# Attention units of a three-kind encoder layer dealt from two streams instead of one

## The chip, the cores and the metric

The kernel runs on one core of one Trainium2 chip. The metric is the device time of one launch in microseconds (us). Before the change the median of three runs is 3494.93 us (3491.45 to 3495.29).

## The reference

Two layers (DEPTH = 2) process a prompt of 1024 tokens and 8 samples of 16 new tokens each, 128 new tokens with 256 past positions a sample: 1152 rows of width 1024. A layer is `x += concat[A(h), B(h), C(h)] @ w_out` with `h = RMSNorm(x)`, and then `x += SwiGLU(RMSNorm(x))`.

One projection of h feeds three kinds of heads, all with normalised q and k:

- A: six query heads on two key/value heads, width 64, a window of the own 64-token chunk and two before it, a learned sink, a bias by distance. Its past is 128 keys.
- B: four differential heads. Each has two softmax maps of width 32; weights are `p0 - lam * p1`; the result is normalised per head. All keys up to the own chunk, a bias by distance, 256 past keys.
- C: six heads, width 64, causal, with cumulative log forget gates added to the scores, 256 past keys.

All arithmetic is float32. The kernel splits operands of its large products into a high and a low part and adds three products.

## The kernel before, in words

After `setup`, a loop over the two layers calls four phases, each with its own tiles, semaphores and a barrier at its end: `project`, `attend`, `mix` and `feed`. The residual x (128 partitions x 9 token tiles x 1024, 4.72 MB) stays in SBUF from `setup` to the end.

`project` (L438) works through 54 units (six column blocks of w_in, nine token tiles each). In each unit PE adds 24 products, ACT squares, DVE norms; two units later PE turns q and k (`turn_rows`), ACT takes the high part out of PSUM (`take_turned`), DVE the low part (`cut_turned`), and SP stores both to `qkT_hi` and `qkT_lo` in DRAM (`store_turned`, L508). The tiles t_hi and t_lo have two buffers each: ACT waits for the stores of two units ago before it writes again. All DMAs of the kernel are issued by SP, in the order of the program.

`attend` (L819) works in groups of two heads: A (three groups), B (two), C (three). A group's head h has nine units, one per token tile; the ninth (i = 8) is the sample tile. So there are 144 units in one row: all of A, all of B, all of C. The engines run in a lock step over iterations u. In iteration u, PE computes the scores of unit u (`score`), turns the weights of unit u-2 (`turn`), turns past keys or finished outputs if any are due (`turn_extra`), multiplies unit u-3 with the values (`values`) and turns a sample's output back (`turn_back`). DVE adds the bias and finds the minimum (`front`), for B also joins the two maps (`back`). ACT takes the exponent (`exps`) and moves what PE turned out of PSUM (`evacuate`, `evacuate_extra`). Each stage has two buffers.

What sets the order of loads is SP's program (L976 to L998): for each group the past keys, past values and sample queries of the next group (`load_past`), then q and k of two heads ahead (`load_qk`, three sets of buffers), then bias rows and values (`load_front`), then the store of the finished group (`mixT`). A wait of SP for a free buffer holds back all that stands behind it. POOL zeroes `qpast` once a group. A's groups j = 0, 1, 2 hold heads j and j+3, so each of the three groups loads and turns the past keys of both key/value heads.

`mix` (L1307) loads, for eight steps g, a stripe of mixT and of w_out, splits them on ACT and DVE, and PE adds step g into eight PSUM banks; then PE does ten more sums with all stripes at hand, and DVE adds the sums to x. The raw tiles have two buffers. `feed` is the gated layer, and takes over half of the time.

Of the kernel before, what the change touches and what calls it, by code (L numbers as in the profile page):

```python
# [437 lines left out]
def project(nc, t, k, layer):  # L438
# [29 lines left out]
    scaled_q, f_sum, f_abs, f_exp, f_ln, f_out, f_stored, rolled = (  # L468
        ph.sem(n) for n in ("scaled_q", "f_sum", "f_abs", "f_exp", "f_ln", "f_out", "f_stored", "rolled"))
# [25 lines left out]
    with nc.Block() as block:  # L495
        @block.sync
        def _(sp):
# [41 lines left out]
            for u, (b, i) in enumerate(work):  # L539
# [27 lines left out]
            sp.wait_ge(rolled, 32)  # L567
            sp.wait_ge(f_stored, 32)
# [217 lines left out]
class Group:  # L786


    def __init__(self, index, kind, j):
        self.index, self.kind, self.j = index, kind, j  # L790
        self.D = B_DIM if kind == "B" else HEAD
        self.maps = P // self.D
        self.per_head = self.maps // 2
        self.packed = P // self.D
        self.nb = DEC_BATCH // self.packed
        self.halves = 1 if kind == "A" else PAST // P
        self.n_past = self.halves * P
        self.n_samp = self.n_past + P
        self.width = 2 * P if kind == "A" else SEQ
        self.tile = {"A": 0, "B": 3, "C": 5}[kind] + j  # L800

        self.q_row = {"A": lambda m: (j + 3 * m) * HEAD, "B": lambda m: 512 + j * P + m * B_DIM,
                      "C": lambda m: 1024 + j * P + m * HEAD}[kind]
        self.k_row = {"A": 384, "B": 768 + j * P, "C": 1408 + j * P}[kind]
        self.v_col = {"A": VA, "B": VB + j * P, "C": VC + j * P}[kind]
        self.past_chunks = self.maps * self.nb * self.halves // 4
# [10 lines left out]


def attend(nc, t, k, layer):  # L819

    ph = Phase(nc, "att")
    groups = [Group(n, kind, j) for n, (kind, j) in enumerate(
        [("A", 0), ("A", 1), ("A", 2), ("B", 0), ("B", 1), ("C", 0), ("C", 1), ("C", 2)])]
    NG, UG = len(groups), 2 * T
    NH = 2 * NG
# [7 lines left out]
    oT, mixTb = ph.sb("oT", [HEAD, P]), ph.sb("mixTb", [P, TOK])

    units = [(g, h, i) for g in groups for h in range(2) for i in range(T)]
    NU = len(units)
    jobs_to = [0]
    for g, h, i in units:
        jobs_to.append(jobs_to[-1] + g.per_head)
    NJ = jobs_to[-1]  # L840
# [6 lines left out]
    sub_sq = ph.sb("sub_sq", [P, T, P])  # L847
    sub_ms, sub_root = ph.sb("sub_ms", [P, UG]), ph.sb("sub_root", [P, UG])
# [3 lines left out]
    add_in, v_in = ([ph.sem(f"{n}{i}") for i in range(2)] for n in ("add_in", "v_in"))  # L852
    kp_in, vp_in, qpast_zeroed, qpast_in, const_in = (
        ph.sem(n) for n in ("kp_in", "vp_in", "qpast_zeroed", "qpast_in", "const_in"))
    prepared, masked, scored, biased, exped, sink_ready, inv_ready, weighed = (
        ph.sem(n) for n in ("prepared", "masked", "scored", "biased", "exped", "sink_ready", "inv_ready", "weighed"))
    turned, evacuated, multiplied, taken_out = (
        ph.sem(n) for n in ("turned", "evacuated", "multiplied", "taken_out"))
    steps, sub_squared, sub_mean, sub_rooted, sub_done, mix_stored = (
        ph.sem(n) for n in ("steps", "sub_squared", "sub_mean", "sub_rooted", "sub_done", "mix_stored"))  # L860

    extra = {}
    for g in groups:
        for c in range(g.past_chunks):
            extra.setdefault(g.index * UG + 2 + c, []).append(("past", g, c))
        for c in range(3):
            extra.setdefault((g.index + 1) * UG + 7 + c, []).append(("mix", g, c))
    N_ITER = NU + 11
    order = []
    for u in range(N_ITER):  # L870
        if 2 <= u <= NU + 1:
            g, h, i = units[u - 2]
            order += [("p", u - 2, c) for c in range(g.n_chunks(i))]
        order += [(what, g.index, c) for what, g, c in extra.get(u, [])]
        if 3 <= u <= NU + 2 and units[u - 3][2] == TP:
            order.append(("new", u - 3, 0))
        if 4 <= u <= NU + 3 and units[u - 4][2] == TP:
# [4 lines left out]
    inv_to = [sum(x[0].kind == "B" or x[2] >= TP - 1 for x in units[:u]) for u in range(NU + 1)]  # L882
    sinks_to = [sum(x[0].kind == "A" and x[2] >= TP - 1 for x in units[:u]) for u in range(NU + 1)]
    n_qk = {"A": 6, "B": 8, "C": 6}
    n_add = {"A": 4, "B": 4, "C": 6}

    def to(g, parity, count):

        return 16 * sum(count(x) for x in groups[:g.index + 1] if parity is None or x.index % 2 == parity)

    def qk_to(hh):

        return 16 * sum(n_qk[groups[x // 2].kind] for x in range(hh % SETS, hh + 1, SETS))

# [3 lines left out]
    def span_of(u):  # L898

        g, h, i = units[u]  # L900
        a = jobs_to[u - i]
        return slice(a, a + TP * g.per_head, g.per_head) if i < TP else slice(jobs_to[u], jobs_to[u] + 1)

    with nc.Block() as block:
        @block.sync
        def _(sp):
# [3 lines left out]
            def load_qk(hh):  # L910

                g, h, b = groups[hh // 2], hh % 2, hh % SETS
                sem, D = qk_in[b], g.D
                if hh >= SETS:
                    sp.wait_ge(scored, jobs_to[(hh - SETS + 1) * T])
                if g.kind == "B":
                    for r, (of_k, of_q) in enumerate(((hi, hi), (lo, hi), (hi, lo), (lo, lo))):
                        own = slice(r * D, (r + 1) * D)
                        for x, src, row in ((0, of_k, g.k_row + 2 * h * D), (1, of_q, g.q_row(2 * h))):
                            sp.dma_start(qk[own, b, x:4:2, :].bitcast(F32), src[row:row + 2 * D, :].rearrange("(m d) n -> d m n", d=D)).then_inc(sem, 16)  # L920
                else:
                    for x, row, parts in ((0, g.k_row + h * D, (hi, lo)), (1, g.q_row(h), (hi, hi)), (2, g.q_row(h), (lo, lo))):
                        for r in range(2):
                            sp.dma_start(qk[r * D:(r + 1) * D, b, x, :].bitcast(F32), parts[r][row:row + D, :]).then_inc(sem, 16)

            def load_front(g):

                b, j, kind, sem = g.index % 2, g.j, g.kind, add_in[g.index % 2]
                if g.index >= 2:
                    sp.wait_ge(biased, jobs_to[(g.index - 1) * UG])  # L930
                for h in range(2):
                    if kind == "A":
                        sp.dma_start(add_p[:, b, h, 0:g.width], t["bias_a"][j + 3 * h]).then_inc(sem, 16)
                        sp.dma_start(add_s[:, b, h, 0:g.n_samp], t["bias_sa"][j + 3 * h]).then_inc(sem, 16)
                    elif kind == "B":
                        sp.dma_start(add_p[:, b, h, :], t["bias_b"][2 * j + h]).then_inc(sem, 16)
                        sp.dma_start(add_s[:, b, h, :], t["bias_sb"][2 * j + h]).then_inc(sem, 16)
                    else:
                        head = slice(2 * j + h, 2 * j + h + 1)
                        sp.dma_start(add_p[:, b, h, :], t["cum_prompt"][head, :].broadcast_to([P, SEQ])).then_inc(sem, 16)  # L940
                        past = t["cum_past"].rearrange("(b h) n -> b h n", h=C_HEADS)[:, head, :]
                        sp.dma_start(add_s[:, b, h, 0:PAST], past.broadcast_to([DEC_BATCH, DEC_SEQ, PAST])).then_inc(sem, 16)
                        sp.dma_start(add_s[:, b, h, PAST:g.n_samp], t["cum_new"][head, :].broadcast_to([P, P])).then_inc(sem, 16)
                if g.index >= 2:
                    sp.wait_ge(multiplied, (g.index - 1) * UG)
# [706 lines left out]
```

## Time and profile before

| what | value |
|---|---|
| median of three runs | 3494.93 us |
| profiled execution | 3499.59 us, span 3498.1 us |
| granted TensorE clock, mean over the span | 0.945 |
| busy: PE, DVE, ACT, POOL | 90%, 46%, 31%, 0% |
| moved by DMA | 335.7 MB, 96 GB/s over the span |

The span is the profiled stretch on the core; the execution's own time is 1.5 us longer. PE's busy time includes pipelined matmuls, so a busy PE is not PE at its peak. The first layer's phases lie at about 80 to 419 us (project), 419 to 822 (attend), 822 to 932 (mix) and from there to about 1780 (feed); the second layer repeats them. The granted clock is TensorE's, as a share of full speed; 1.00 is 2.4 GHz, 0.50 is 1.2 GHz.

### The profile page before, as it was taken

The page shows a single profiled execution, that of the slowest core. Times are in us where ns is not written, and L with a number is a line of the kernel's source. Part 1 is how long each engine was busy: PE and PEld are TensorE (multiplying, and loading weights), DVE is VectorE, ACT ScalarE, POOL GpSimd, SP SyncE. Part 2 cuts the span into 40 slices and gives each one's busy share as a digit, 9 for nine tenths or more (in the row PEclk, how much of TensorE's full clock was granted, in tenths as well). Part 3 has the DMA queues.
Part 4 walks back from the last instruction along what each step waited for, and adds up shares of the span by engine and source line. Part 5 has one row for each costly group of instructions (what it writes and reads, how often), then busy time and mean ns, then how long its engine had stood idle before and what let it go on. Part 6 is the DMA issues. An engine that isn't in the chain of part 4 may idle for free. (4 is left out here: it accounts for less than half of the span.)

```text
span 3498.1 us, 48824 instructions
## 1 busy us (share of the span) xinstructions
PE 3143.7 (90%) x17938; PEld 2884.2 (82%) x17938; DVE 1592.4 (46%) x3178; ACT 1070.4 (31%) x2279; POOL 15.4 (0%) x20
## 2 busy tenths in 40 slices
PE   0699788898899999999968996889898999999999
PEld 0588787787799999999957896778777999999998
DVE  0455236633244545445446452483234454454454
ACT  1332166663321111111123223576524111111112
POOL 0000000000000000000000000000000000000000
PEclk9899878998999999999989998789998999999999
DMA  7255586753021111111024557866322111111111
GB/s 171 86 173 160 174 201 151 184 131 116 20 65 36 54 36 36 54 36 36 24 90 145 162 185 173 183 161 152 108 82 67 37 36 54 36 36 54 36 36 61
DMA packets 417475, 335.70 MB, mean 96 GB/s; under 512 B 132578, under 2 KB 376238, under 8 KB 417274
## 3 DMA queue, kind: packets, MB, share of 16 engines
q1 hardware_dynamic: 417306, 333.53, 35.1%
q8 instruction: 96, 1.57, 0.2%
q14 instruction: 73, 0.60, 0.1%
HBM read 238.31 MB, written 96.97 MB: 96 GB/s over the span
## 5 line engine op out<-in xcount | busy, mean ns | idle before, releaser
L1560 DVE TENSOR_TENSOR x<-x,ffn_down 128x512 f32<-128x512 f32 x792 | 509.5, 683 | 0.0
L1582 DVE TENSOR_TENSOR ffn_xn<-ffn_xn,ffn_up 128x384 f32<-128x384 f32 x132 | 73.1, 554 | 758.0 <-ACT ffn_xn L1527 758.0
L408 PE MATMUL ffn_up<-ffn_h_hi,ffn_hi_g 128*128 128x384 f32 x1056 | 360.5, 341 | 15.0 <-DVE ffn_h_lo L233 10.4
L410 PE MATMUL ffn_up<-ffn_h_hi,ffn_lo_g 128*128 128x384 f32 x1056 | 359.8, 341 | 0.0
L409 PE MATMUL ffn_up<-ffn_h_lo,ffn_hi_g 128*128 128x384 f32 x1056 | 359.2, 340 | 0.0
L408 PE MATMUL ffn_up<-ffn_h_hi,ffn_hi_u 128*128 128x384 f32 x1056 | 355.3, 336 | 3.2 <-DVE ffn_lo_u L233 3.2
L410 PE MATMUL ffn_up<-ffn_h_hi,ffn_lo_u 128*128 128x384 f32 x1056 | 354.9, 336 | 0.0
L409 PE MATMUL ffn_up<-ffn_h_lo,ffn_hi_u 128*128 128x384 f32 x1056 | 354.9, 336 | 0.0
L1527 ACT ACTIVATE ffn_xn<-ffn_up 128x384 f32<-128x384 f32 x132 | 64.9, 491 | 861.1 <-PE ffn_up L410 861.1
L408 PE MATMUL prj_acc<-prj_w_hi,prj_h_hi 128*128 128x384 f32 (+2 forms) x864 | 322.1, 373 | 3.1 <-DVE prj_w_lo L233 3.0
L409 PE MATMUL prj_acc<-prj_w_lo,prj_h_hi 128*128 128x384 f32 (+2 forms) x864 | 312.4, 362 | 0.0
L410 PE MATMUL prj_acc<-prj_w_hi,prj_h_lo 128*128 128x384 f32 (+2 forms) x864 | 311.9, 361 | 0.0
L408 PE MATMUL ffn_down<-ffn_hi_d,ffn_a_hi 128*128 128x512 f32 x792 | 308.3, 389 | 0.0
L409 PE MATMUL ffn_down<-ffn_lo_d,ffn_a_hi 128*128 128x512 f32 x792 | 308.2, 389 | 0.0
L410 PE MATMUL ffn_down<-ffn_hi_d,ffn_a_lo 128*128 128x512 f32 x792 | 308.2, 389 | 0.0
L1034 PE MATMUL att_S<-att_qk 128*128 128x256 f32 (+3 forms) x672 | 196.8, 394 | 72.3 <-DMA att_qk<-scratch_qkT_lo 55.9
L1097 PE MATMUL att_O<-att_vn,att_pT 128*128 128x64 f32 x1800 | 250.8, 284 | 0.0
L1141 ACT ACTIVATE att_p<-att_s,att_bias 128x128 f32<-128x128 f32 (+3 forms) x360 | 241.9, 674 | 13.9 <-DVE att_bias L1238 12.8
L1238 DVE CUSTOM_DVE_ANT_0 att_s<-att_S,att_add_p 128x128 f32<-128x128 f32 (+3 forms) x224 | 164.8, 755 | 178.5 <-PE att_S L1037 123.9
L1097 PEld LDWEIGHTS att_O<-att_vn,att_pT 128*128 128x128 f32 x1800 | 245.9, 209 | 0.0
L1155 ACT ACTIVATE att_pT<-att_TR 128x256 f32<-128x256 f32 (+3 forms) x368 | 158.3, 453 | 197.5 <-PE att_TR L1059 195.5
L408 PEld LDWEIGHTS ffn_up<-ffn_h_hi,ffn_hi_g 128*128 128x128 f32 x1056 | 202.5, 192 | 18.4 <-DVE ffn_h_lo L233 11.6
(172 smaller groups left out, 5156.3 us busy)
## 6 DMA issues: line engine op xcount, KB each, us to landing
att_qk<-scratch_qkT_hi SPq DMA_DIRECT2D x104, 288.0 KB, 6.6
att_qk<-scratch_qkT_lo SPq DMA_DIRECT2D x104, 288.0 KB, 8.5
ffn_raw_g<-in_w_gate SPq DMA_DIRECT2D x44, 512.0 KB, 4.0
ffn_raw_u<-in_w_up SPq DMA_DIRECT2D x44, 512.0 KB, 5.1
ffn_raw_d<-in_w_down SPq DMA_DIRECT2D x44, 512.0 KB, 5.0
scratch_qkv<-prj_nat SPq DMA_DIRECT2D x72, 192.0 KB, 1.9
prj_w_raw<-in_w_in SPq DMA_DIRECT2D x64, 192.0 KB, 2.7
scratch_qkv<-prj_nat SPq DMA_DIRECT2D x36, 256.0 KB, 2.1
```

What stands on the lines that cost most here:

```text
L408: pe.matmul(out, l_hi, r_hi, start=first, stop=False)
L409: pe.matmul(out, l_hi, r_lo, start=False, stop=False)
L410: return pe.matmul(out, l_lo, r_hi, start=False, stop=final)
L1034: last = pe.matmul(out[:, c:c + w], q, kk[:, k0 + c:k0 + c + w], start=(x == 0), stop=(x == len(qs) - 1 and not masked_end))
L1097: last = pe.matmul(O[:, hh % 2, i * HEAD:(i + 1) * HEAD], pT[:, u % 2, x * P:(x + 1) * P], vn[:, b, kt, v], start=(x == 0), stop=(x == len ...
L1141: act.activation(p[:, u % 2, r, 0:n], s[:, job % 2, 0:n], ACT.Exp, bias=bias[:, job:job + 1], scale=-1.0, accum_out=total[:, job:job + 1]) ...
L1155: act.activation(pT[:, u % 2, c * 512:c * 512 + w], TR[:, n % 2, 0:w], ACT.Copy).then_inc(evacuated, 1)
L1238: dve.tensor_tensor_reduce(s[:, job % 2, 0:n], S[:, job % 2, 0:n], extra_row, -1.0, lowest, ALU.add, ALU.min, bias[:, job:job + 1]).then_i ...
L1527: act.activation(sg[:, b, :], up[:, b, 0, 0:384], ACT.Silu).then_inc(activated, 1)
L1560: dve.tensor_tensor(x, x, down[:, (q * ND + n) % 4, :], ALU.add).then_inc(added, 1)
L1582: dve.tensor_tensor(a32[:, b, :], sg[:, b, :], up[:, b, 1, 0:384], ALU.mult).then_inc(gated, 1)
```

## The change

- `Group` becomes `Head`: 16 heads, 0 to 5 of A, 6 to 9 of B, 10 to 15 of C. Heads 2p and 2p+1 form pair p, whose output is one stripe of mixT. A's pairs are neighbours now, so mixT has the order of the reference, and w_out is loaded in one piece in every step of `mix`.
- `two_streams` deals the 144 units: stream 0 holds A's 54, stream 1 B's 36 and then C's 54. Each unit has a weight; the units are sorted by the share of their stream's weight that lies ahead of them.
- A's six heads form one bundle: values, past keys and past values are loaded once, and past keys turned once in a layer. B and C have a bundle per pair. The turned past keys (`kpT`), past values (`vp`), output columns (`O`) and `mixn` have one place a stream, the raw past keys (`kp`) and `mixTb` one in all; q and k still have three sets. `qpast` has four, and is zeroed once in a layer.
- For A and C, the low part of q is multiplied with the high part of k alone (64 rows); the low-by-low product and its load are left out.
- SP's order is planned: each load is listed at the unit whose end frees its buffer (-1: at once), and the loads of one unit are sorted by the unit that needs them.
- vn, mixn, sub_sq and mixTb lie in x's place in SBUF. `project` stores x to DRAM in unit 9, `mix` loads it back after the loads of step 6.

```diff
+        t["x_kept"] = nc.dram_tensor("scratch_x_kept", (P, T, D_MODEL), F32).ap()
...
                 if u >= 1 and NORMED[work[u - 1][0]]:
                     store_turned(order[u - 1])
+                if u == T:
+                    sp.dma_start(t["x_kept"], k["x"][:]).then_inc(x_kept, 16)
...
+    def weight(self, i):
+
+        return 3.5 * self.halves if i == TP else self.n_cols(i) / P * 0.45 + 0.1
+
+
+def two_streams(heads):
+
+    order = []
+    for stream in range(2):
+        own = [(h, i) for h in heads if h.stream == stream for i in range(T)]
+        whole, at = sum(h.weight(i) for h, i in own), 0
+        for h, i in own:
+            order.append((at / whole, stream, h, i))
+            at += h.weight(i)
+    order.sort(key=lambda e: e[:2])
+    return [(h, i) for _, _, h, i in order]
...
+    spare = k["x"][:].rearrange("p t d -> p (t d)")
+    vn = spare[:, 0:4 * TOK].rearrange("p (s t d) -> p s t d", s=4, t=T)
+    mixn = spare[:, 4 * TOK:6 * TOK].rearrange("p (s t d) -> p s t d", s=2, t=T)
...
+    for h in openers:
+        past_at[h.n] = max(at[h.n, 1], after)
+        after = past_at[h.n] + h.past_chunks + 2
...
+    for h in seconds:
+        mix_at[h.n] = after = max(end[h.n] + 8, after)
...
+    for h in begun:
+        load_at.setdefault(free_at(qk_before[h.n]), []).append((first[h.n], 0, "qk", h))
+        load_at.setdefault(free_at(add_before[h.n]), []).append((first[h.n], 1, "add", h))
+        load_at.setdefault(free_at(q_before[h.n]), []).append((end[h.n], 3, "qpast", h))
+    for n, h in enumerate(openers):
+        v_last = None if v_before[h.bundle] is None else closer[v_before[h.bundle]]
+        load_at.setdefault(free_at(v_last) + 3 * (v_last is not None), []).append((first[h.n], 2, "v", h))
+        kp_free = -1 if n == 0 else past_at[openers[n - 1].n] + openers[n - 1].past_chunks - 1
+        load_at.setdefault(kp_free, []).append((past_at[h.n], 4, "kp", h))
+        vp_last = None if past_before[h.bundle] is None else closer[past_before[h.bundle]]
+        load_at.setdefault(free_at(vp_last) + 3 * (vp_last is not None), []).append((end[h.n], 5, "vp", h))
+    for h in seconds:
+        load_at.setdefault(mix_at[h.n] + 2, []).append((N_ITER, 6, "mix", h))
...
-                    for x, row, parts in ((0, g.k_row + h * D, (hi, lo)), (1, g.q_row(h), (hi, hi)), (2, g.q_row(h), (lo, lo))):
+                    for x, row, parts in ((0, h.k_row, (hi, lo)), (1, h.q_row, (hi, hi)), (2, h.q_row, (lo,))):
...
+                        passes = [(qk[:, b, 1, tok], qk[:, b, 0, :]), (qk[0:HEAD, b, 2, tok], qk[0:HEAD, b, 0, :])]
...
+                    if c == 0 and pair_rank[h.pair]:
+                        act.wait_ge(mix_stored, 16 * pair_rank[h.pair])
...
+                sp.dma_start(w_raw[:, g % 2, :], src[g * P:(g + 1) * P, :]).then_inc(came[g % 2], 16)
+                if g == KD - 2:
+                    sp.dma_start(k["x"][:], t["x_kept"]).then_inc(x_in, 16)
...
+            dve.wait_ge(x_in, 16)
             for u in range(2 * T):
```

## Rows read from the trace of the kernel before

**Rows 1.** Windows by stage: stretch, length, busy by engine, granted clock, DMA share, GB/s.
```profile
429.00:545.00 116.00, 90.28 (x620) 84.53 (x621) 39.90 (x169) 64.97 (x219) 2.85 (x3) 0.75 0.87 199
545.00:649.00 104.00, 91.35 (x623) 79.04 (x622) 81.21 (x215) 73.87 (x183) 0.95 (x1) 0.88 0.74 169
649.00:805.00 156.00, 149.53 (x1228) 134.22 (x1227) 59.48 (x156) 99.58 (x234) 2.86 (x3) 0.98 0.54 131
```
**Rows 2.** Windows of single heads: A, B, B with past keys, two of C.
```profile
447.25:457.23 9.98, 9.98 (x94) 9.66 (x94) 5.46 (x24) 8.58 (x32) 0.38 (x1) 1.00 1.06 252
630.22:656.42 26.20, 23.58 (x183) 19.77 (x183) 22.20 (x64) 20.03 (x54) 0.95 (x1) 1.00 0.76 189
596.87:630.22 33.35, 27.69 (x206) 24.04 (x206) 28.91 (x71) 25.76 (x62) 0.00 (x0) 0.95 0.56 120
711.05:759.50 48.45, 47.37 (x403) 42.79 (x403) 15.32 (x44) 30.52 (x75) 0.95 (x1) 1.00 0.71 173
...
640.00:650.00 10.00, 8.16 (x46) 5.49 (x46) 9.72 (x26) 8.39 (x20) 0.00 (x0) 1.00 0.97 251
```
**Rows 3.** Timeline of PE in attention: start, length, line, operation, count, [idle before, releaser].
```profile
435.77 0.80 PE L1034 MATMUL att_S<-att_qk 128*128 128x256 f32 x2 [5.36 <-DVE att_bias L1238]
...
528.35 0.47 PE L1034 MATMUL att_S<-att_qk 128*128 128x128 f32 x2
...
537.25 1.09 PE L1073 MATMUL att_TR<-ident,att_kp 128*128 128x128 f32 x4 [5.22 <-DMA att_kp<-in_cache_b_k]
```
**Rows 4.** Waits, 419 to 822 us: total, times, longest.
```profile
PE att_S L1034 <- DMA att_qk<-scratch_qkT_lo: 28.3, 4, 14.6
```
**Rows 5.** Window of attention's first loads.
```profile
420.00:460.00 40.00, 23.97 (x180) 22.59 (x180) 12.71 (x56) 20.30 (x68) 0.95 (x1) 0.71 1.05 234
```
**Rows 6.** Timeline of SP's queue in attention.
```profile
418.93 0.54 SPq L924 DMA_DIRECT2D att_qk<-scratch_qkT_hi  x1
...
524.36 10.16 SPq L959 DMA_DIRECT2D att_kp<-in_cache_b_k  x8
```
**Rows 7.** DMA issues: count, KB each, median us from issue to landing.
```profile
att_qk<-scratch_qkT_lo SPq DMA_DIRECT2D x104, 288.0 KB, 8.5
...
x<-in_x_prompt SPq DMA_DIRECT2D x1, 4096.0 KB, 13.6
...
scratch_bias_b<-set_tile_b SPq DMA_DIRECT2D x1, 2048.0 KB, 8.7
```
**Rows 8.** Timeline of all engines at the end of attention.
```profile
806.10 0.56 DVE L1238 CUSTOM_DVE_ANT_0 att_s<-att_S,att_add_s 128x384 f32<-128x384 f32 x1 [2.45 <-PE att_S L1045]
...
817.99 0.77 ACT L1168 ACTIVATE att_mixTb<-att_TR 128x512 f32<-128x512 f32 x2 [0.26 <-PE att_TR L1082]
818.77 0.35 SPq L997 DMA_DIRECT2D scratch_mixT<-att_mixTb  x1
822.45 0.32 SPq L1337 DMA_DIRECT2D mix_m_raw<-scratch_mixT  x1
```
**Rows 9.** Timeline of SP's queue in the projection, units 9 and 10.
```profile
209.71 0.65 SPq L517 DMA_DIRECT2D scratch_qkT_lo<-prj_t_lo  x1
...
213.28 0.58 SPq L517 DMA_DIRECT2D scratch_qkT_lo<-prj_t_lo  x1
```
**Rows 10.** Timeline of ACT in the projection.
```profile
220.47 0.38 ACT L228 ACTIVATE prj_t_hi<-prj_turn 128x256 fp32r<-128x256 f32 x1 [1.14 <-DMA scratch_qkT_lo<-prj_t_lo]
...
222.10 0.38 ACT L650 ACTIVATE prj_sq<-prj_acc 128x256 f32<-128x256 f32 x1 [1.15 <-PE prj_acc L410]
...
226.56 0.38 ACT L650 ACTIVATE prj_sq<-prj_acc 128x256 f32<-128x256 f32 x1 [2.48 <-PE prj_acc L410]
```
**Rows 11.** Timeline of ACT in mix, step 7.
```profile
861.51 1.17 ACT L228 ACTIVATE mix_m_hi<-mix_m_raw 128x1152 fp32r<-128x1152 f32 x1 [0.99 <-DMA mix_w_raw<-in_w_out]
```
**Rows 12.** Timeline of DVE in mix, step 7 and the first sums.
```profile
863.99 1.22 DVE L233 TENSOR_TENSOR mix_w_lo<-mix_w_raw,mix_w_hi 128x1024 fp32r<-128x1024 f32 x1
873.02 5.45 DVE L1382 TENSOR_TENSOR x<-x,mix_acc 128x512 f32<-128x512 f32 x8 [7.81 <-PE mix_acc L410]
```

More of the change, by code:

```diff
@@ L819, in attend @@
 def attend(nc, t, k, layer):
     ph = Phase(nc, "att")
[L822 to L825, printed above, removed]
-    SETS = 3
+    heads = [Head(n) for n in range(A_HEADS + B_HEADS + C_HEADS)]
+    units = two_streams(heads)
+    NU, NP = len(units), len(heads) // 2
+    at = {(h.n, i): u for u, (h, i) in enumerate(units)}
+    first, end = ({h.n: at[h.n, i] for h in heads} for i in (0, TP))
@@ new lines, in attend, with rotate @@
+    begun = sorted(heads, key=lambda h: first[h.n])
+    ended = sorted(heads, key=lambda h: end[h.n])
+    openers = [h for h in begun if h.first_of_bundle]
+    closer = {h.bundle: h for h in heads}
+    SETS = 3
+    jobs_to = [0]
+    for h, i in units:
+        jobs_to.append(jobs_to[-1] + h.maps)
+    NJ = jobs_to[-1]
+    column = [sum(T * x.maps for x in heads[:h.n]) + i * h.maps for h, i in units]
+    def rotate(users, slots, start, stop):
+        place, before, last = {}, {}, [None] * slots
+        for x in users:
+            s = min(range(slots), key=lambda s: -1 if last[s] is None else stop(last[s]))
+            place[x.n], before[x.n], last[s] = s, last[s], x
+            assert before[x.n] is None or stop(before[x.n]) < start(x)
+        return place, before
@@ L832, in attend @@
+    qpast = ph.sb("qpast", [P, 4, 4, P])
+    add_p, add_s = ph.sb("add_p", [P, 4, SEQ]), ph.sb("add_s", [P, 4, 3 * P])
     s, p, pT = ph.sb("s", [P, 2, SEQ]), ph.sb("p", [P, 2, 2, SEQ]), ph.sb("pT", [P, 2, SEQ])
[L833 to L840, printed above, removed]
+    oT = ph.sb("oT", [HEAD, P])
@@ L862, in attend @@
[L862 to L865, printed above, removed]
-        for c in range(3):
-            extra.setdefault((g.index + 1) * UG + 7 + c, []).append(("mix", g, c))
-    N_ITER = NU + 11
+    steps, sub_mean, sub_rooted, sub_done, mix_stored = (
+        ph.sem(n) for n in ("steps", "sub_mean", "sub_rooted", "sub_done", "mix_stored"))
+    seconds = [h for h in ended if h.half]
+    extra, sub_at, load_at = {}, {}, {}
@@ L871, in attend @@
         if 2 <= u <= NU + 1:
[L872 to L875, printed above, removed]
+            h, i = units[u - 2]
+            order += [("p", u - 2, c) for c in range(h.n_chunks(i))]
+        order += [(what, h.n, c) for what, h, c in extra.get(u, [])]
+        if 3 <= u <= NU + 2 and units[u - 3][1] == TP:
             order.append(("new", u - 3, 0))
-        if 4 <= u <= NU + 3 and units[u - 4][2] == TP:
+        if 4 <= u <= NU + 3 and units[u - 4][1] == TP:
             order.append(("back", u - 4, 0))
@@ L881, in attend @@
     weighed_to = [sum(x[0].kind == "B" for x in units[:u]) for u in range(NU + 1)]
[L882 to L893, printed above, removed]
+    inv_to = [sum(x[0].kind == "B" or x[1] >= TP - 1 for x in units[:u]) for u in range(NU + 1)]
@@ new lines, in attend, with in_slot @@
+    sinks_to = [sum(x[0].kind == "A" and x[1] >= TP - 1 for x in units[:u]) for u in range(NU + 1)]
+    taken_to = {h.n: m + 1 for m, h in enumerate(sorted(heads, key=lambda h: at[h.n, TP - 1]))}
+    pair_rank = {h.pair: m for m, h in enumerate(seconds)}
+    sub_rank = {h.pair: m for m, h in enumerate(x for x in seconds if x.kind == "B")}
+    n_qk = {"A": 5, "B": 8, "C": 5}
+    n_add = {"A": 2, "B": 2, "C": 3}
+    def in_slot(users, slot_of, x, count):
+        upto = [y.n for y in users].index(x.n) + 1
+        return 16 * sum(count(y) for y in users[:upto] if slot_of(y) == slot_of(x))
@@ new lines, in load_vp @@
+            def load_vp(h):
+                before = past_before[h.bundle]
+                if before is not None:
+                    sp.wait_ge(multiplied, end[closer[before].n] + 1)
+                src = t[f"cache_{h.kind.lower()}_v"][layer].rearrange("b p h d -> p b (h d)")
+                cols = slice(0, P) if h.kind == "A" else slice(h.j // 2 * P, (h.j // 2 + 1) * P)
+                for f in range(h.halves):
+                    sp.dma_start(vp[:, h.stream, f, :, :], src[f * P:(f + 1) * P, :, cols]).then_inc(vp_in[h.stream], 16)
@@ L978, in _, with store_mix, loads @@
+            def store_mix(h):
+                sp.wait_ge(evacuated, place["mix", h.n, 2] + 1)
+                sp.dma_start(t["mixT"][h.pair * P:(h.pair + 1) * P, :], mixTb).then_inc(mix_stored, 16)
+            def loads(u):
+                for _, _, what, h in sorted(load_at.get(u, []), key=lambda e: e[:2] + (e[3].n,)):
+                    {"qk": load_qk, "add": load_add, "v": load_v, "kp": load_kp, "vp": load_vp,
+                     "qpast": load_qpast, "mix": store_mix}[what](h)
             sp.dma_start(mask_f[:], t["c_causal"]).then_inc(const_in, 16)
@@ new lines, in score @@
+                        for c in range(h.nb):
+                            x = m * h.nb + c
+                            pe.matmul(out[:, 0:h.n_past], qpast[:, q_set[h.n], r * h.nb + c, :],
+                                      kpT[:, h.stream, x * h.n_past:(x + 1) * h.n_past], start=(c == 0), stop=(c == h.nb - 1))
+                        for x, (q, kk) in enumerate(passes):
+                            last = pe.matmul(out[:, h.n_past:h.n_samp], q, kk[:, SEQ:TOK], start=(x == 0), stop=(x == len(passes) - 1))
@@ L1318, in mix @@
     src = t["w_out"][layer]
[L1319 removed]
+    x_in = ph.sem("x_in")
     def came_by(g):
[L1323 removed]
+        return 32 * (g // 2 + 1)
     def product(pe, u, g):
```

492 lines of the change are left out of this document (246 added, 246 removed).

## Prediction

> **What bounds the kernel now.** Read the stage table first, since a mean over the span mixes stages with different limits [rows 1]. Columns: stretch, its length, busy time of PE, PEld, DVE, ACT, POOL, granted clock, DMA share, GB/s. Attention of the first layer runs from 418.9 to 822.4 us. Its A stretch (116 us) has a granted clock of 0.75 and DMA at 0.87: PE waits for loads, then works at the lower of its two levels. In the B stretch DVE is busy 81 of 104 us. In the C stretch PE is busy 149.5 of 156 us at clock 0.98: nothing but PE bounds it.
>
> Then take clean heads, without waits for data [rows 2]. An A head takes 9.98 us, PE busy throughout. The last B head takes 26.2 us with DVE busy 22.2; inside it, from 640 to 650 us, DVE is busy 9.72 of 10. A B head with past keys to turn takes 33.35. Two C heads with everything take 48.45, PE 47.4. So clean A work is 6 x 9.98 = 60 us; A really takes from 435.77, when its scores start in earnest [rows 3], to 528.35, where B's first scores stand, some 93 us. What alternation could recover is those 33 us and 10 to 15 us of waits in B and C (PE waits 28.3 us for q and k in this layer, 14.6 of them ahead of the first score [rows 4]).
>
> **The attention core, part by part (one layer).** All instructions stay but four groups of four past-key turns of A with their evacuations (2 x 0.6 us each in PE, some 2.4 us, in the sum through A's price); PE issues as many score passes as before, the low-q pass with 64 rows for 128. 6.6 MB of loads go (A's values, past keys and past values twice, one 288 KB piece for each of 12 heads). POOL's eight memsets become one; PE never waited for them directly, so I cost them at nothing.
>
> *B section.* By the dealing rule (an A head weighs 11.05, a B or C head 24), C begins at unit 59, after 36 B units and 23 A units (2.55 heads). B: 4 x 26.2 = 104.8, and twice 33.35 - 26.2 = 7.15 for the past keys, mix turns and norm: 119. The A units cost between DVE's price, 2.55 x 5.46 = 14, where DVE is what is short, and their full 2.55 x 9.98 = 25; B's small units are PE's, its large ones DVE's, so I take the middle, 19. Sum 138, bounds 133 and 145. If the engines overlapped without loss, DVE's busy time, 2 x (22.20 + 28.91) + 14 = 116, would be the floor [rows 2].
>
> *C section.* 3 x 48.45 = 145.4; the other 31 A units 3.44 x 9.98 = 34.4; two mix turns, 3. That is 183, and 186 with 2% for the lock step (PE's idle share in C now). Bounds 183 and 200.
>
> *The start.* Here the change adds a wait. SP issues in order, and all that has a free buffer goes first: constants 0.14 MB, A head 0's q and k 1.47, its bias 0.26, values 0.59, B head 6's q and k 2.36, bias 0.72, values 0.59, A's past keys 0.52, past values 1.05, head 7's q and k 2.36 and bias 0.72, A's past values 0.52, one more bias 0.26, values 0.59. Only then come B's past keys, 1.05 MB, because the one past-key buffer must first be turned for A. Together 13.2 MB. At the start DMA runs full at 234 GB/s [rows 5]: 56.4 us, with 1 us to the first landing 57.4. SP's own issue gives the same: some 57 DMAs at 0.4 to 0.6 us, then 10.16 us for those eight [rows 6]. PE needs them in iteration 8. Without that wait it would be there after 5.54 MB (23.7 us, plus latency: 25) and 13 us of work (three A units, five small B units) at 38 to 40 us. So PE stands some 18 us, and values, turns and scores stand behind the turn in PE's queue. Before, the first B head waited 5.22 us for the same data [rows 3]. I add 2 us for the lower clock after it. Bounds: 4 us, at the 309 GB/s of x's first load (4.2 MB in 13.6 us [rows 7]), and 28, at the 199 GB/s of the A stretch [rows 1].
>
> *Loads in flight.* Three q-and-k sets for two running heads leave one ahead. Counting units between the release and the first use, all heads have 8 or more but A head 3, with 4 (units 69 to 73, some 8 us of C work): five issues of 0.6 us and 8.5 us to landing [rows 7] make 11.5, so a 3 us wait.
>
> Core: 57.4 + 2 + (138 - 13) + 186 + 3 = 373.4 us to the last unit's scores. Before, from 418.93 [rows 6] to 806.10 [rows 8]: 387.2. **Gain 13.8 us.**
>
> *The tail.* A's last pair and C's last pair end two units apart, at 141 and 143, and share one mixTb. The store of the first runs as now, issued at 818.77, landed at 822.45; only then may ACT evacuate the second (0.77 us for its last two chunks, some 1.4 for all three) and SP store it (3.7) [rows 8]. Now there is one. **+5 us.**
>
> **x out (projection).** 4.72 MB are stored by SP in unit 9. x loads at 13.6 us for 4.2 MB, a 2.1 MB store took 8.7 [rows 7]: between 14 and 20 us, I take 17. Behind it stand t_hi and t_lo stores, nat stores and weight loads. That queue is late already: the t_lo store issued at 209.71 was waited for until 220.47, behind small gate loads [rows 9, 10]. The next, at 213.28, now lands at 220.5 + 17 = 237.5. ACT stands at the evacuation of turned rows from 222.4 on, and in ACT's queue the next square and root stand behind it. PE, at 4.45 us a unit (squares at 222.10 and 226.56 [rows 10]), does two units more, to 230.7, and starts again some 3 us after 237.5. **+10 us**, bounds 3 and 14.
>
> **x back (mix).** SP issues x behind the weights of step 6 and ahead of step 7. Step 7's weights landed at 861.51 [rows 11] and were cut at 865.2; PE turned to step 7 at 872.2, as the first sum is added at 873.02 [rows 12]: 7 us to spare. With 14 us of x ahead it is cut at 879.3. 7 us late, 8 to 10 with the lower clock after it: **+10 us**, bounds 0 and 15. The single w_out load for steps 0 to 2 in place of two gains under 1 us. DVE's new wait for x costs nothing: x lands before step 7 does.
>
> The Trainium skill, page "DMA: Bandwidth & Descriptors", section "Queues, rings and completion order", says that each DMA engine consumes descriptors in ring order. It speaks against both copies: they are placed on the one queue ahead of what PE needs next. The late store at 220.47 agrees [rows 10]. If a later small transfer could pass a large one, both terms would be 0 (second rival).
>
> **Sum.** A layer: -13.8 + 5 + 10 + 10 = +11.2; two layers +22.4. Against the profiled execution's 3499.6 us (span 3498.1) that is 3522.0; the median of the runs, 3494.9, lies 4.7 lower: **3517 us**. My own range for this case is 3490 to 3550.
>
> **Rivals.** *1. The streams fill each other (faster).* The B section falls to its floor of 116 and the start hides its wait: 39 + (116 - 13) + 183 = 325, gain 62; less 25 is 37 a layer: 3421. For: A and C keep PE full [rows 2]. Against: B alone leaves DVE 4 of 26 us idle in the same lock step. Chance 15%.
> *2. The copies are hidden.* Both x terms 0: -13.8 + 5 = -8.8 a layer: 3477. For: PE has 7 us spare in mix and two units of cover in the projection. Against: the store waited for until 220.47 [rows 10]. Chance 18%.
> *3. Alternation itself costs (slower still).* Each short unit is followed by a long one in a two-deep lock step, so PE waits for ACT's exponent or evacuation; A units pay their full price in B (+6), C runs at 200 (+14), and late q and k add 10: +30 a layer, 3577. It decides where an A unit between two C units takes over 1.4 us. For: ACT is busy 8.58 of 9.98 in A, 20 of 26 in B [rows 2]. Against: C has 18 us of ACT spare in 48. Chance 17%.
>
> The forecast has the remaining 50%. No change that can be told is within 0.2%, 7 us. Faster: rival 1, most of rival 2 and the forecast's edge, 31%. Same: 10%. Slower: 59%. Range 3440 to 3580, which reaches to the middle of rivals 1 and 3.
>
> **What would show it.** Right: one idle stretch of PE of 10 to 25 us some 40 us into attention, ended by a past-key load of B; no own A stretch, clock near 1 from there on; last scores 360 to 380 us after the first issue; PE idle 5 to 13 us in the projection, ended through a t_lo store; idle 5 to 12 us in mix ahead of the last step; two mixT stores one after the other at the end. Wrong: attention shorter by over 40 us, no PE idle behind either copy of x, or a C section over 200 us.

## The result and the profile after

The changed kernel takes **3748.64 us** (3731.57 to 3763.91, four runs) against 3495.11 us (3491.45 to 3495.84): a ratio of 1.0726, 95% interval 1.0672 to 1.078. Forecast was 3517, range 3440 to 3580. The profiled execution has a span of 3756.2 us, 258 more than before, at a mean granted clock of 0.902 (0.945 before). The feed-forward phase, some 49% of the time before (two stretches of some 857 us), is no slower, so the difference lies ahead of it.

First the windows by stage of the changed kernel, first layer. Columns as in [rows 1]: stretch, length, busy PE, PEld, DVE, ACT, POOL, granted clock, DMA share, GB/s. The stretches are: projection; attention until B's scores begin; the first units and the wait for B's past keys; the B section; the C section to the last scores; the tail; mix (from 952.5).

```profile
80.00:427.00 347.00, 290.14 (x1530) 262.81 (x1530) 159.78 (x391) 94.47 (x214) 0.00 (x0) 0.94 0.49 153
...
427.10:453.00 25.90, 0.88 (x2) 0.57 (x2) 1.30 (x7) 1.78 (x3) 1.76 (x1) 0.50 0.90 193
453.00:494.00 41.00, 13.34 (x64) 10.46 (x64) 12.31 (x43) 11.37 (x34) 0.00 (x0) 0.62 0.98 205
494.00:644.70 150.70, 134.27 (x888) 116.25 (x888) 97.47 (x274) 97.22 (x259) 0.00 (x0) 0.86 0.56 122
644.70:932.00 287.30, 283.85 (x1492) 224.52 (x1491) 70.03 (x214) 123.23 (x330) 0.00 (x0) 0.69 0.36 83
932.00:952.50 20.50, 13.76 (x116) 11.94 (x115) 1.54 (x5) 6.47 (x16) 0.00 (x0) 0.72 0.15 58
...
952.00:1065.00 113.00, 100.24 (x432) 82.23 (x432) 32.31 (x35) 27.42 (x35) 0.00 (x0) 0.94 0.32 121
```

Attention starts at 427.1 and mix at 952.5: 525.4 us against 403.5 before (418.93 to 822.45, [rows 6, 8]), or +122 a layer. The projection is 8 us longer; mix is as long as before. Over two layers that makes 260, about the 258 us.

The C section takes 287.3 us where 186 was forecast, and PE is busy in 283.9 of them. So it isn't a wait. The granted clock is 0.69. The next fence shows where it falls: the same columns, from 684 us on.

```profile
684.00:690.00 6.00, 5.70 (x52) 4.82 (x51) 1.46 (x5) 3.06 (x10) 0.00 (x0) 1.00 1.03 226
690.00:693.00 3.00, 3.00 (x36) 2.31 (x35) 0.03 (x2) 0.87 (x3) 0.00 (x0) 0.82 0.87 218
693.00:707.00 14.00, 14.00 (x47) 9.87 (x47) 3.08 (x10) 5.71 (x16) 0.00 (x0) 0.50 0.02 3
707.00:735.00 28.00, 28.00 (x102) 22.50 (x102) 4.89 (x13) 8.40 (x21) 0.00 (x0) 0.50 0.00 1
735.00:738.00 3.00, 3.00 (x18) 2.32 (x16) 0.57 (x2) 1.11 (x3) 0.00 (x0) 0.78 0.19 29
738.00:752.00 14.00, 14.00 (x120) 11.91 (x120) 5.37 (x20) 8.48 (x27) 0.00 (x0) 1.00 1.08 262
```

PE never stands from 690 to 752, and yet the clock goes from 1.00 (2.4 GHz) to 0.50 (1.2 GHz) in the middle, and stays there for over 40 us. What PE did at the fall, in the timeline of PE (start, length, line, operation, count): small products of a sample tile, and then score passes, turns and values in the usual mix. Each pair of scores (x2) is a 128-row pass and a 64-row one.

```profile
689.87 1.99 PE L1208 MATMUL att_TR<-att_pT,att_vp 128*64 128x16 f32 x32
691.79 1.21 PE L1134 MATMUL att_S<-att_qk 128*128 128x384 f32 x2
...
693.98 1.09 PE L1134 MATMUL att_S<-att_qk 128*128 128x256 f32 x2
```

What the fall costs is read from PE's groups by form, between 672 and 687 us (upper three rows) and between 693 and 735 us (lower three): busy time, then mean ns of one. A 64-row pass takes as long as one of 128 rows, at either level.

```profile
L1197 PE MATMUL att_O<-x,att_pT 128*128 128x64 f32 x44 | 5.5, 269 | 0.0
L1134 PE MATMUL att_S<-att_qk 64*128 64x512 f32 x2 | 1.0, 496 | 0.0
L1134 PE MATMUL att_S<-att_qk 128*128 128x512 f32 x2 | 1.0, 489 | 0.0
...
L1197 PE MATMUL att_O<-x,att_pT 128*128 128x64 f32 x70 | 16.1, 404 | 0.0
L1134 PE MATMUL att_S<-att_qk 64*128 64x512 f32 x6 | 4.8, 793 | 0.0
L1134 PE MATMUL att_S<-att_qk 128*128 128x512 f32 x6 | 4.7, 777 | 0.0
```

At the lower level everything takes 1.5 to 1.6 times as long (404 against 269, 793 against 496).

The rows that answer to [rows 3]: PE's timeline at the start, with the idle time before each in brackets.

```profile
439.61 0.88 PE L1134 MATMUL att_S<-att_qk 128*128 128x128 f32 x2 [16.98 <-DMA att_qk<-scratch_qkT_lo]
453.70 0.69 PE L1134 MATMUL att_S<-att_qk 128*128 128x128 f32 x2 [13.21 <-DMA att_qk<-scratch_qkT_lo]
...
494.93 1.09 PE L1173 MATMUL att_TR<-ident,att_kp 128*128 128x128 f32 x4 [24.49 <-DMA att_kp<-in_cache_b_k]
```

To [rows 9, 10], SP's issue and ACT's wait in the projection:

```profile
208.67 0.56 SPq L554 DMA_DIRECT2D scratch_x_kept<-x  x1
...
213.63 1.26 SPq L518 DMA_DIRECT2D scratch_qkT_lo<-prj_t_lo  x1
```

```profile
226.22 0.38 ACT L229 ACTIVATE prj_t_hi<-prj_turn 128x256 fp32r<-128x256 f32 x1 [12.68 <-DMA scratch_qkT_lo<-prj_t_lo]
```

To [rows 11, 12], steps 6 and 7 of mix on ACT, then DVE's first sum:

```profile
984.48 1.17 ACT L229 ACTIVATE mix_m_hi<-mix_m_raw 128x1152 fp32r<-128x1152 f32 x1 [3.29 <-DMA mix_w_raw<-in_w_out]
...
998.47 1.17 ACT L229 ACTIVATE mix_m_hi<-mix_m_raw 128x1152 fp32r<-128x1152 f32 x1 [11.88 <-DMA mix_w_raw<-in_w_out]
```

```profile
1003.30 5.39 DVE L1479 TENSOR_TENSOR x<-x,mix_acc 128x512 f32<-128x512 f32 x8 [1.13 <-PE mix_acc L411]
```

And to [rows 8], the two mixT stores at the end:

```profile
944.48 4.67 SPq L1086 DMA_DIRECT2D scratch_mixT<-x  x2
947.36 1.44 ACT L1269 ACTIVATE x<-att_TR 128x512 f32<-128x512 f32 x3 [2.90 <-DMA scratch_mixT<-x]
952.51 0.33 SPq L1436 DMA_DIRECT2D mix_m_raw<-scratch_mixT  x1
```

### The profile page after: what moved, and what is told of

It reads as the page before. It is cut to its first block and busy times, and to the rows that moved or that the text cites. A ratio compares the mean times of both kernels' runs of the same rounds, so it can differ in the third digit from the quotient of the medians.

```text
span 3756.2 us, 48690 instructions
## 1 busy us (share of the span) xinstructions
PE 3350.4 (89%) x17906; PEld 2993.9 (80%) x17906; DVE 1593.1 (42%) x3178; ACT 1063.6 (28%) x2271; POOL 3.8 (0%) x6
## 5 line engine op out<-in xcount | busy, mean ns | idle before, releaser
L1134 PE MATMUL att_S<-att_qk 128*128 128x256 f32 (+7 forms) x672 | 296.3, 501 | 69.7 <-DMA att_qk<-scratch_qkT_lo 60.2
L1197 PE MATMUL att_O<-x,att_pT 128*128 128x64 f32 x1800 | 293.3, 316 | 0.0
L1197 PEld LDWEIGHTS att_O<-x,att_pT 128*128 128x128 f32 x1800 | 291.3, 242 | 0.0
L1134 PEld LDWEIGHTS att_S<-att_qk 128*128 128x128 f32 (+1 forms) x672 | 153.1, 237 | 155.1 <-issue 62.0
L1241 ACT ACTIVATE att_p<-att_s,att_bias 128x256 f32<-128x256 f32 (+7 forms) x360 | 241.7, 673 | 37.1 <-DVE att_bias L1337 34.9
```

Source lines behind the costliest of these rows:

```text
L1134: last = pe.matmul(out[:, c:c + w], q, kk[:, k0 + c:k0 + c + w], start=(x == 0), stop=(x == len(passes) - 1 and not masked_end))
L1197: last = pe.matmul(O[:, h.stream, i * HEAD:(i + 1) * HEAD], pT[:, u % 2, x * P:(x + 1) * P], vn[:, b, kt, v], start=(x == 0), stop=(x == l ...
L1241: act.activation(p[:, u % 2, r, 0:n], s[:, job % 2, 0:n], ACT.Exp, bias=bias[:, col:col + 1], scale=-1.0, accum_out=total[:, col:col + 1]) ...
```

## Experiments: which part lowers the clock

Theory N: the 64-row second passes of A and C lower the granted clock. Rival D: the alternation does, by short units between long ones and sample tiles close together. Three runs each undo or do one part alone.

**128-row passes back in the changed kernel.**

```diff
-    n_qk = {"A": 5, "B": 8, "C": 5}
+    n_qk = {"A": 6, "B": 8, "C": 6}
...
-                    for x, row, parts in ((0, h.k_row, (hi, lo)), (1, h.q_row, (hi, hi)), (2, h.q_row, (lo,))):
+                    for x, row, parts in ((0, h.k_row, (hi, lo)), (1, h.q_row, (hi, hi)), (2, h.q_row, (lo, lo))):
...
-                        passes = [(qk[:, b, 1, tok], qk[:, b, 0, :]), (qk[0:HEAD, b, 2, tok], qk[0:HEAD, b, 0, :])]
+                        passes = [(qk[:, b, 1, tok], qk[:, b, 0, :]), (qk[:, b, 2, tok], qk[:, b, 0, :])]
```

> The changed kernel with the second score pass of A and C on 128 rows again (low-by-low product and its load back); all else stays. Theory N (the 64-row passes let the granted clock fall to 0.50 while PE is busy without a gap): the C section of the changed kernel spends some 180 us of attention at 0.50, where the same products take about 1.55 times as long (value products 406 ns against 268), so some 65 us a layer come back: 3749 - 130 = about 3620 us, and the clock in the C section is 0.95 or more. Theory D (dealing the units in alternation, with its sample tiles close together, makes the clock fall or PE wait): no gain, 3745 to 3765 us, clock in the C section below 0.75 as in the changed kernel.

Measured: 3549.37 us, ratio to before 1.0154 (1.0124 to 1.0185): 199 us come back, more than the 130 forecast. Its windows by stage, cut as above (start, first units and wait, B, C, tail):

```profile
429.10:456.00 26.90, 0.69 (x2) 0.50 (x2) 1.30 (x7) 1.78 (x3) 1.80 (x1) 0.50 0.91 197
456.00:497.50 41.50, 12.88 (x64) 10.34 (x64) 12.30 (x43) 11.40 (x34) 0.00 (x0) 0.62 1.00 202
497.50:636.80 139.30, 120.89 (x888) 108.36 (x888) 97.33 (x272) 97.29 (x258) 0.00 (x0) 0.90 0.62 136
636.80:828.50 191.70, 183.44 (x1500) 167.69 (x1499) 70.75 (x218) 122.78 (x332) 0.00 (x0) 0.95 0.61 139
828.50:847.60 19.10, 12.40 (x111) 10.48 (x110) 1.10 (x5) 6.44 (x16) 0.00 (x0) 0.76 0.16 63
```

C's section falls from 287.3 to 191.7 us and its clock rises from 0.69 to 0.95; B's, with 23 A units in it, from 150.7 to 139.3. Start, wait and tail stay. That is 107 us of the 122. The clock falls at times with 128 rows too, but for less long: by the granted clocks of these rows and of the ones above, an estimate, B and C together spend some 47 us at the lower level with 128 rows and some 220 with 64.

**64-row passes alone, in the kernel before** (the same three edits, the other way).

> The kernel before, with the 64-row second pass for A and C as the only edit (one 288 KB load less for each of 12 heads). Theory N: A's and C's stretches lose clock although PE is busy; if 60% of the C stretch runs at 0.50, 156 us become about 197, and A adds some 10: about +50 us a layer, 3560 to 3640 us. Theory D: nothing but fewer loads changes, 3480 to 3500 us, C stretch at clock 0.98.

Measured: 3636.65 us, ratio 1.0382 (1.0321 to 1.0442). Nothing is dealt here, x is copied nowhere, and fewer bytes are moved; A's stretch and C's alone get slow, B's does not. Its windows for A, B and C (upper three rows), and those of the kernel before in the same cuts, from the first scores of a kind to the next kind's (lower three):

```profile
436.00:557.00 121.00, 116.30 (x545) 96.11 (x545) 29.92 (x125) 53.49 (x185) 1.90 (x2) 0.61 0.64 148
557.00:681.80 124.80, 109.95 (x734) 94.30 (x734) 96.75 (x266) 88.80 (x223) 2.86 (x3) 0.87 0.66 149
681.80:884.00 202.20, 198.05 (x1186) 154.60 (x1186) 52.88 (x140) 91.47 (x220) 1.91 (x2) 0.81 0.38 93
...
436.00:528.00 92.00, 77.33 (x556) 73.89 (x557) 30.34 (x130) 56.56 (x191) 1.94 (x3) 0.78 0.88 205
528.00:656.00 128.00, 109.20 (x727) 93.96 (x726) 96.07 (x265) 87.79 (x221) 2.83 (x3) 0.87 0.69 156
656.00:806.00 150.00, 144.18 (x1191) 129.69 (x1191) 52.69 (x138) 93.87 (x223) 1.90 (x2) 0.98 0.55 135
```

C's 202.2 us at clock 0.81 stand against 150 at 0.98, A's 121 at 0.61 against 92 at 0.78. B's 124.8 stand against 128, both at 0.87. The cuts of [rows 1] lie up to 17 us away from the first scores of B and C, so its lengths don't compare with these.

**The changed kernel's units in one row**, 64-row passes kept:

```diff
-    order.sort(key=lambda e: e[:2])
+    order.sort(key=lambda e: e[1])
```

> The changed kernel with the units in one row (all of A, then B, then C) by one changed sort key; the 64-row pass, the planned loads and the copies of x stay. Theory N: A's and C's stretches still fall to 0.50 while PE is busy; 3600 to 3700 us. Theory D: attention is as long as before the change or shorter, and only the copies of x remain: 3500 to 3530 us, clock in C's stretch 0.95 or more.

Measured: 3660.37 us, 1.0452 (1.0405 to 1.0499). Without alternation the clock is low all the same: rival D falls as the main cause, N stands.

**Rows, or what they hold?** The lower 64 rows of q's low part are zeros, read from a DRAM tensor:

```diff
-                    for x, row, parts in ((0, h.k_row, (hi, lo)), (1, h.q_row, (hi, hi)), (2, h.q_row, (lo,))):
+                    for x, row, parts in ((0, h.k_row, (hi, lo)), (1, h.q_row, (hi, hi)), (2, h.q_row, (lo, None))):
...
-                            sp.dma_start(qk[r * D:(r + 1) * D, b, x, :].bitcast(F32), part[row:row + D, :]).then_inc(sem, 16)
+                            sp.dma_start(qk[r * D:(r + 1) * D, b, x, :].bitcast(F32), t["zero"] if part is None else part[row:row + D, :]).then_inc(sem, 16)
...
-                        passes = [(qk[:, b, 1, tok], qk[:, b, 0, :]), (qk[0:HEAD, b, 2, tok], qk[0:HEAD, b, 0, :])]
+                        passes = [(qk[:, b, 1, tok], qk[:, b, 0, :]), (qk[:, b, 2, tok], qk[:, b, 0, :])]
```

> As the run with 128-row second passes (3549 us), but the lower 64 rows of the low part of q are zeros, loaded in place of the low part (one copy of 0.29 MB between DRAM tensors more in the projection): the result is that of the 64-row pass, the array runs on 128 rows. If the rows that a matmul spans decide, the clock stays up as with the low part: 3540 to 3565 us. If what the rows hold decides, zeros are as bad as 64 rows: 3700 to 3760 us.

Measured: 3545.01 us, 1.0138 (1.0115 to 1.016). The product is that of the 64-row pass, the time that of the 128-row one: how many rows a matmul spans decides, not the numbers in them. Every kernel with 64-row passes also loads one 288 KB piece less for each such head, and no run separates the two. What speaks against a part of the loads is that PE is busy without a gap while the clock is low, and DMA moves 3 GB/s or less in the rows from 693 to 735 us.

## Experiments: what is left, and a faster version

With 128 rows the change still costs 51 us (3549.37 less 3498.69, the kernel before run beside it). Each of the next three runs starts from that kernel, the later ones from what these show.

**Past keys in the order in which bundles end**, B's first:

```diff
-    openers = [h for h in begun if h.first_of_bundle]
+    openers = sorted([h for h in begun if h.first_of_bundle], key=lambda h: end[h.n])
-        past_at[h.n] = max(at[h.n, 1], after)
+        past_at[h.n] = max(5 if not past_at else 17 if h.kind == "A" else at[h.n, 1], after)
```

> As the run with 128-row second passes, and the past keys come in the order in which their bundles end: B's first (turned in iterations 5 to 8), then A's (from iteration 17). Theory O (order alone makes PE stand 25 us for B's past keys): the stand goes or falls to 5 us, some 20 us a layer: about 3510 us (3500 to 3525). Rival T (the first 13 MB are late as a whole, DMA is full at some 195 GB/s): the wait turns up at the next load, the values, A's past keys or head 7's q and k; 3535 to 3550 us.

Measured: 3516.64 us, 1.0063 (1.0049 to 1.0076), 33 us less. PE's wait for B's past keys, in its timeline:

```profile
467.38 1.09 PE L1173 MATMUL att_TR<-ident,att_kp 128*128 128x128 f32 x4 [2.38 <-DMA att_kp<-in_cache_b_k]
```

**x stored in nine pieces**, units 9 to 17:

```diff
-                if u == T:
-                    sp.dma_start(t["x_kept"], k["x"][:]).then_inc(x_kept, 16)
+                if T <= u < 2 * T:
+                    sp.dma_start(t["x_kept"][:, u - T, :], k["x"][:, u - T, :]).then_inc(x_kept, 16)
```

> As the run with 128-row second passes, and x is stored in nine pieces of 0.52 MB, one in each of the projection's units 9 to 17, in place of one of 4.72 MB in unit 9. If the one block ahead of the t_lo store costs the 8 to 10 us by which the projection is longer, 14 to 18 us of the two layers come back: about 3533 us. If it is the bytes (DMA has no room there), 3545 to 3555 us.

Measured: 3529.55 us, 1.0095 (1.0081 to 1.0109), 20 us less; attention starts at 418.8, as before the change. The bytes were not the cost, the one block ahead of a store was.

**One row of units, 128-row passes** (the changed sort key and the three edits):

> As the run with 128-row second passes, but the units in one row (all of A, then B, then C). It shows what alternation itself is worth once the clock stays up. If alternation costs (two heads' q and k before steady work, two streams' first loads): 3510 to 3535 us, the copies of x being all that is left. If it gains in B and C what A's loads cost: 3555 to 3580 us.

Measured: 3475.30 us, 0.9945 (0.9933 to 0.9958): faster than both kernels, and below both ranges that were expected. So alternation costs 74 us here, while the rest of the change gains; which part of it (planned loads, A's past keys turned once, fewer loads) no run separates. In its trace one wait stands out, DVE's in A's stretch (total, times, longest):

```profile
DVE att_s L1337 <- DMA att_add_s<-scratch_bias_sa: 20.0, 2, 19.3
```

A's third head waits for its bias. Ahead of it in SP's order stands all that is listed "at once", B's first loads among it.

**One row, x in nine pieces, loads listed no earlier than 24 units ahead** (for all six kinds of load):

```diff
-        load_at.setdefault(free_at(add_before[h.n]), []).append((first[h.n], 1, "add", h))
+        load_at.setdefault(max(-1, free_at(add_before[h.n]), first[h.n] - 24), []).append((first[h.n], 1, "add", h))
...
```

> One row of units with 128-row second passes (3475 us), plus x stored in nine pieces, plus loads listed no earlier than 24 units ahead of the unit that needs them (so the bias of A's third head is no longer behind B's first loads; DVE waited 19.3 us for it). If both edits add up: 3475 - 20 - 2 x 15 = 3425 us (3415 to 3440). Rival: DMA is full through A's stretch (231 GB/s), the wait only moves to the next head's q and k: 3445 to 3458 us.

Measured: **3429.19 us**, 0.9821 (0.9804 to 0.9838), the best version: 65 us faster than the kernel before.

**The same, with 64-row passes for A alone**, where A waits for loads:

> As the run before in this list, but A alone has the 64-row second pass, without the load of the lower half (6 x 288 KB a layer less). Theory N: A's stretch runs partly at 0.50 and gets longer: 10 to 30 us a layer slower than with 128 rows. Rival: A waits for DMA anyway, 1.7 MB less at 231 GB/s is 7 us a layer: 10 to 15 us faster in all.

Measured: 3489.46 us, 0.9997 (0.9984 to 1.001): 60 us slower than with 128 rows, though it loads 1.8 MB less a layer. Rows of A's stretch from the end of its first units to B's first scores, 128 rows first, then 64:

```profile
447.00:505.30 58.30, 54.34 (x450) 51.66 (x450) 25.73 (x109) 42.95 (x154) 0.00 (x0) 0.89 1.01 230
```

```profile
447.00:546.00 99.00, 99.00 (x489) 82.57 (x489) 27.82 (x117) 46.60 (x165) 0.00 (x0) 0.64 0.73 160
```

This is the whole case in two rows: PE busy 99.00 of 99 us, nothing waited for, and 41 us lost. (The rows don't hold quite the same matmuls, since less was done before 447 us; from 417 us to B's first scores it is 129 us against 88.3, again 41.) The profiled execution is the slowest of its twelve, 3517.96 us; by the medians A alone loses 30 us a layer.

**Alternation with all that helped** (128 rows, past keys by end, x in nine, loads 24 ahead):

> Alternation with all that has helped: 128-row passes, B's past keys first, x in nine pieces, loads at most 24 units ahead. If the gains add up: 3517 - 20 = 3497 us, and the later listing may take another 5 us a layer from the start: 3480 to 3500 us, still 50 us or more above the same kernel with the units in one row. If only the order of loads was wrong with alternation, it comes down to the one row's time, 3425 to 3445 us.

Measured: 3495.45 us, 1.0001 (0.9988 to 1.0014): back at the kernel before, 66 us above the row. Its windows (start, B, C), and the row's (start with A's first units, the rest of A, B, C):

```profile
417.00:445.00 28.00, 0.69 (x2) 0.50 (x2) 1.30 (x7) 1.78 (x3) 1.80 (x1) 0.50 0.88 191
445.00:615.50 170.50, 143.68 (x951) 127.40 (x952) 109.56 (x315) 108.53 (x292) 0.00 (x0) 0.82 0.76 160
615.50:808.50 193.00, 184.70 (x1499) 168.87 (x1499) 70.73 (x218) 122.65 (x332) 0.00 (x0) 0.94 0.59 138
```

```profile
417.00:447.00 30.00, 11.82 (x78) 11.15 (x78) 5.52 (x25) 9.85 (x31) 1.80 (x1) 0.60 0.92 207
...
505.30:620.30 115.00, 102.25 (x749) 86.37 (x749) 97.11 (x267) 89.45 (x227) 0.00 (x0) 0.95 0.83 183
620.30:770.30 150.00, 143.75 (x1187) 129.21 (x1187) 52.11 (x139) 93.56 (x221) 0.00 (x0) 0.98 0.51 128
```

In its first 28 us the dealt kernel does 0.69 us of matmuls, since it wants two heads' q and k before any steady work; the row does 11.8 in 30. In its second stretch, A and B in turn, the clock is 0.82, against 0.95 in the row's B; why it is lower no run shows. DVE is busy there 109.6 us of 170.5, so it isn't the bound that it is in the row's B (97.1 of 115). All in all the three stretches are 38 us longer than the row's four (391.5 against 353.3): PE's busy time has 17 of them, its idle time 21, and 9 of these lie in the start.

**Alternation in B's stretch alone** (A's last three heads among B's units):

> As the best version with the units in one row (3429 us), but A's last three heads are dealt among B's units; A's first three heads stay in a row ahead, C in a row behind. Start and C's stretch are those of the row, so only alternation where DVE is the bound is left. If what alternation lost was the start with two heads' loads: B's stretch leaves PE 12.75 us idle of 115, A's units fill them, 5 to 12 us a layer: 3405 to 3420 us. If it loses in B too, since PE stands shortly between units and the granted clock falls with it (0.82 in the B section of the dealt kernel, 0.95 in the row): 10 to 25 us a layer slower, 3450 to 3480 us.

Measured: 3514.85 us, 1.006 (1.0045 to 1.0074): 86 us slower than the row, beyond both expectations. A and B together take 220.9 us against 188.3, C 165.1 against 150.0. The first two rows are this kernel's, the last two the row's.

```profile
431.00:651.90 220.90, 179.13 (x1266) 160.76 (x1265) 127.10 (x395) 139.69 (x403) 0.00 (x0) 0.84 0.77 166
651.90:817.00 165.10, 149.59 (x1199) 133.65 (x1199) 53.05 (x141) 95.55 (x228) 0.00 (x0) 0.93 0.51 125
```

```profile
432.00:620.30 188.30, 167.58 (x1271) 148.35 (x1271) 127.41 (x396) 142.25 (x410) 0.00 (x0) 0.91 0.91 203
620.30:770.30 150.00, 143.75 (x1187) 129.21 (x1187) 52.11 (x139) 93.56 (x221) 0.00 (x0) 0.98 0.51 128
```

Of A and B's 32.6 us, PE's busy time (the same matmuls, more of them at 1.2 GHz) has 11.5 and its idle time 21. PE's timeline splits the idle time. Late loads have some 14 us: 8.8 for q and k, where the row has none, and 9.5 for the bias of an A head, through DVE, where the row has 3.9. Waits for the weights that DVE joins have 9 (15.2 against 6.4). C's stretch is not the row's either, though its order is: PE stands 8.9 us at 695.9 for an evacuation by ACT, which waits 10.6 us for a store to mixT. So this run doesn't isolate alternation where DVE is the bound. What it shows of that is the 9 us and a lower clock; the rest is what the new order did to loads and stores.

## Why the prediction was wrong

**The step that failed** is half a sentence: "PE issues as many score passes as before, the low-q pass with 64 rows for 128", costed at nothing. By duration that holds (496 ns against 489). What it missed is the granted clock: with these passes it falls to 0.50 while PE is busy without a gap, and the other matmuls near them take 1.5 to 1.6 times as long (404 ns against 269, 777 against 489). The runs put it at 199 us (taken out of the changed kernel), 138 us (alone in the kernel before: 3636.65 less 3498.69, with the gain of fewer loads in it), and 60 us (A alone). I had looked for the clock only behind waits ("clock near 1 from there on"), since in the kernel before low stretches go with waits [rows 1]; no rival held a fall without one. One of the signs named for "wrong" did show: a C section over 200 us.

The Trainium skill, page "TensorE: Matmul & The Clock Gate", section "Part 1: The HAM clock gate", says that activity releases the throttle; A's stretch at 0.64 with PE busy 99.00 of 99 us shows that a PE which is busy in the profile can still be throttled. The same page, section "Why this matters for your kernels", says that one matmul on 32 rows takes the same time as one on 128; for 64 rows the durations here agree (496 ns against 489).

The other steps are read from the run with 128-row passes, first layer:

- *Start.* One stand of PE, ended by B's past keys, as forecast: 25 us (25.27, and 24.49 in the changed kernel) against 18. It ended 69.6 us after attention's start (429.1 to 498.7), not 57.4: in the 68.4 us of the two rows DMA moved some 13.7 MB at 200 GB/s (197 and 202), where I had 13.2 at 234. So the rate was mis-sized, down to the lower bound of 199. SP's issue did not "give the same" either: 57 issues at 0.4 to 0.6 us and 10.16 us make 33 to 44 us, not 57. SP reached B's first past key 60 us after the start (488.87), and two of its issues ahead of it took 14.76 and 8.71 us. The cause, the order of loads, is shown: 33 us for two layers come back when B's past keys go first.
- *B section.* Forecast 125 us behind the wait (138 less 13), measured 139.3: mis-sized by 14, and over the upper bound (145 less 13). The clock of 0.90 is part of it.
- *C section.* 186 plus 3 us for a late q and k, 191.7 measured, with one wait of 1.3 us for q and k: right.
- *Core.* 399.4 us to the last scores (429.1 to 828.5) for 373.4: instead of 13.8 us gained, 12 lost.
- *Tail.* +5 forecast, 19.1 us against 16.5 (806 to 822.5): +2.6. The second evacuation did wait for the first store (2.90 us).
- *x out.* +10 forecast; the projection ends 8 us later here and 10 in the run with 128 rows, through the t_lo store named (ACT waits 12.68 us for it). The mechanism is right, and shown by the nine pieces; the size is partly luck. With two buffers, the store issued at 209.71 before the change was waited for until 214.64, and the one at 213.28 until 218.57; 220.47 belongs to a later one. In the changed kernel that second store (issued at 213.63) was there at 226.2, not 237.5, and PE stood from 220.2 on, not 230.7: both some 10 us early, so that the difference came out.
- *x back.* +10 forecast, 0 measured: mix takes 112.3 us (952.5 to 1064.8). x did push step 7 back, 14 us behind step 6 (998.47, 984.48; before 3 us, 861.51 [rows 11] and 858.4). So x took 11 us, not 14. And step 6 landed 32 us after mix began (952.5), not 36 (822.4), so the slack was 7 plus 4 us: just enough. The first sum comes 51 us after mix began in both kernels [rows 12].

With 128 rows, then, the sum is +12 +3 +10 +0 = +25 a layer for a forecast of 11, and 3549 us for 3517. That it is no further off is luck too: the 10 us that x back did not cost hide part of the 26 by which the core was mis-sized. (The loads that go are 6.8 MB a layer, not 6.6; no term hangs on it.) Rival 3, "alternation itself costs", was therefore the right direction for what is left: the row beats the dealt units by 66 to 74 us. Its mechanism, PE waiting for ACT between C units, is not what shows: C's section is near the forecast. What shows is the start with two heads' loads and a lower clock where A and B alternate; what lowers it there stays open. Rival 1, that the streams fill each other, falls with the same runs.

## What to carry to other kernels

Leaving out half the rows of a matmul saved no time in it here (496 ns against 489), and with such passes in A's and C's scores the clock of all the matmuls around them fell to half for long stretches: pad with real or zero rows up to 128, and compare the granted clock of the stretch. When PE is busy throughout and a stretch is still too long, look at the clock column and at the mean ns of a matmul that wasn't changed. Dealing two kinds of work in turn means that the loads of two heads, not one, must have landed before the first steady work; check the start before the overlap.

## What was unexpected of the hardware

- The granted clock falls without any gap of PE: 1.00 to 0.50 at 692 us, and back only at 736, PE busy throughout.
- Rows of zeros keep it up as well as rows of data (3545 and 3549 us, 3749 with 64 rows).
- 4.72 MB to or from DRAM in one transfer took 15.7 to 15.9 us from issue to landing, for estimates of 17 and 14; cut into nine pieces in nine units, the store cost the projection nothing (attention starts at 418.8, as before the change).
